# Input rows loaded at once, the residual's store moved, output rows straight from the residual

## The reference

```python
h = x + concat(rmsnorm(fox), rmsnorm(conv), rmsnorm(nsa), rmsnorm(gmlp)) @ w_out
y = h + square(relu(rmsnorm(h) @ w_ff1)) @ w_ff2
```

## Time and profile before

| | |
|---|---|
| median of the runs | 3586.47 us (3577.64, 3598.64, 3586.47) |
| the profiled execution | 3587.85 us, its span 3586.0 us |
| mean granted TensorE clock | 0.972 of full |
| busy: TensorE, VectorE, ScalarE, GpSimd | 3298.0, 1469.9, 1019.8, 206.5 us |
| the first barrier | TensorE's first product at 59.26 us |
| the last barrier | VectorE's first copy behind it at 3563.27 us |

### The profile page before, as it was taken

How to read it: one execution, slowest core, us unless ns; L and a number is a source line. 1 busy time by engine, 2 the same in 40 slices (tenths; PEclk the granted TensorE clock), 3 DMA queues, 4 the chain that set the end, 5 groups by cost and what they waited for, 6 DMA issues and landing times.

```text
span 3586.0 us, 55381 instructions
## 1 busy us (share of the span) xinstructions
PE 3298.0 (92%) x22246; PEld 1888.7 (53%) x22450; DVE 1469.9 (41%) x2767; ACT 1019.8 (28%) x1802; POOL 206.5 (6%) x136
## 2 busy tenths in 40 slices
PE   5999978888799999999989998889887999999998
PEld 3555556666544444444445554566664444444444
DVE  4875553333454321232168665433335533113321
ACT  2112334444433210221102232344444332013211
POOL 0211100000100000000002111000002000000000
PEclk9999979999999999999999998999998999999999
DMA  6432242342221121123143324334222112111322
GB/s 192 153 102 76 90 150 85 120 142 69 78 92 47 54 58 41 41 58 90 48 138 107 101 76 127 111 107 137 103 84 90 47 53 65 47 30 47 81 75 79
DMA packets 379859, 313.02 MB, mean 87 GB/s; under 512 B 125597, under 2 KB 362810, under 8 KB 372538
## 3 DMA queue, kind: packets, MB, share of 16 engines
q1 hardware_dynamic: 372234, 209.13, 20.7%
q0 software_dynamic: 7424, 101.19, 7.6%
HBM read 264.87 MB, written 50.46 MB: 88 GB/s over the span
## 4 chain that ended last, share of the span: by engine, by line
PE 82%; DVE 6%; ACT 3%; SPq 3%; issue 3%; DMA 2%; POOL 0%; POOLq 0%; DVEq 0%; ACTq 0%
PE PS L943 43%; PE PS L1058 10%; PE PS L1318 5%; PE PS L1339 4%; PE PS L972 3%; PE PS L1209 3%; PE PS L1033 2%; PE PS L1357 1%; PE PS L1388 1%; PE PS L1255 1%; DVE arena L1890 1%; ACT arena L1622 1%; PE PS L1216 1%; DVE arena L2179 1%; PE PS L1108 1%
## 5 line engine op out<-in xcount | busy, mean ns | idle before, releaser
L943 PE MATMUL PS<-arena 128*128 128x512 bf16 (+1 forms) x9882 | 1538.7, 316 | 10.4
L943 PEld LDWEIGHTS PS<-arena 128*128 128x128 bf16 x10080 | 753.4, 98 | 794.7
L1058 PE MATMUL PS<-arena 128*128 128x512 f32 (+3 forms) x1152 | 477.6, 570 | 0.0
L1499 ACT ACTIVATE arena<-arena 128x1024 bf16<-128x1024 f32 (+1 forms) x112 | 145.4, 1300 | 1095.7 <-PE PS L943 1075.4
L1058 PEld LDWEIGHTS PS<-arena 128*128 128x128 f32 (+1 forms) x1152 | 208.3, 184 | 236.6 <-issue 203.6
L2460 DVE TENSOR_TENSOR arena<-PS,arena 128x1088 f32<-128x1088 f32 (+1 forms) x48 | 62.0, 1292 | 654.8 <-PE PS L943 631.4
L2184 DVE TENSOR_REDUCE arena<-PS 128x1 f32<-128x1024 f32 (+5 forms) x192 | 138.8, 724 | 368.2 <-PE PS L1321 367.6
L1318 PE MATMUL PS<-arena 128*128 128x512 f32 (+3 forms) x576 | 236.6, 519 | 10.5 <-ACT arena L1631 8.8
L2484 DVE SCALAR_TENSOR_TENSOR arena<-PS,arena 128x1088 f32<-128x1088 f32 x64 | 82.7, 1292 | 350.9 <-PE PS L943 350.5
L1339 PE MATMUL PS<-arena 128*128 128x64 f32 x1632 | 215.9, 278 | 0.0
L1339 PEld LDWEIGHTS PS<-arena 128*128 128x128 f32 x1632 | 203.8, 197 | 8.4 <-issue 5.2
(11 more groups left out here) (334 smaller groups left out, 2880.7 us busy)
## 6 DMA issues: line engine op xcount, KB each, us to landing
arena<-in_w_ff SPq DMA_DIRECT2D x64, 512.0 KB, 4.1
arena<-in_w_ff SPq DMA_DIRECT2D x32, 1024.0 KB, 5.9
arena<-in_cache_nsa_kv SPq DMA_DIRECT2D x256, 64.0 KB
x_s<-arena SPq DMA_DIRECT2D x24, 544.0 KB, 3.5
arena<-x_s SPq DMA_DIRECT2D x2, 4352.0 KB, 12.9
arena<-in_w_in SPq DMA_DIRECT2D x4, 2048.0 KB, 14.5
arena<-in_w_out SPq DMA_DIRECT2D x16, 512.0 KB, 4.0
arena<-in_w_in SPq DMA_DIRECT2D x12, 512.0 KB, 5.8
```

What stands on the lines that cost most here:

```text
L943: last = mm(PS[:, 1536 * k + a:1536 * k + a + wd], ww[:, c, :], xx[:, c, a:a + wd], start=c == 0 and n == 0, stop=c == blocks - 1 and n == 2)
L1058: last = mm(PS[0:r, c * 512:c * 512 + b - a], XNT[:, j, t * P:t * P + r], Wt[:, j, a:b], start=j == 0, stop=j == KD - 1)
L1499: run(WH[k][:, 0:blocks, :], src[k][:, 0:blocks, :], ACT.Copy).then_inc(S["w_hi"], 1)
```

## The change

- Nine buffers `XS` take the two `XS` and the two `XO`. The input tiles are issued without a wait: tiles 0 to 3 right behind the constants, tiles 4 to 8 behind the page table's DMAs. `quad_s` is written first among these and read back after tile 8. The norm gains and the four gate weights follow.
- The constants have a semaphore of their own, `const_in`, on which TensorE and VectorE begin. `loaded_once` (288) is waited for by GpSimd and by VectorE's index tables, which now stand behind the reductions of the squares.
- SP arrives at the first barrier before it stores the residual; the eight stores are the first that it issues behind it.
- At the end TensorE transposes directly out of `XT` into four pairs of PSUM banks. ScalarE evicts the first half of a tile, VectorE the second (`row_odd`), and SP stores the tile out of its own buffer. No store is waited for before the last.

```diff
-        XS = [lo.take(DM) for _ in range(2)]
-        XO = [lo.take(KD * P, k=KD, n=P) for _ in range(2)]
+        XS = [lo.take(DM) for _ in range(QT + 1)]
...
         def _(sp):
-            sp.dma_start(const, A["consts"]).then_inc(loaded_once, 16)
+            sp.dma_start(const, A["consts"]).then_inc(const_in, 16)
+
+            def row_in(t):
+                src = A["x_prompt"][0, t * P:(t + 1) * P, :] if t < QT else A["x_sample"].rearrange("b t d -> (b t) d")
+                sp.dma_start(XS[t][0:P if t < QT else NS, :], src).then_inc(S[f"row_in{t}"], 16)
+
+            for t in range(4):
+                row_in(t)
+            sp.dma_start(quad_s.unsqueeze(2), ...).then_inc(quad_out, 16)
             sp.dma_start(pages, A["page_table"].rearrange("b j -> (b j)").unsqueeze(0)).then_inc(loaded_once, 16)
-
             for j in range(NPG):
                 r = slice(j * (P // NPG), (j + 1) * (P // NPG))
                 sp.dma_start(block_rows[r, :], ...).then_inc(loaded_once, 16)
-            sp.dma_start(quad_s.unsqueeze(2), ...).then_inc(quad_out, 16)
+            for t in range(4, QT + 1):
+                row_in(t)
             sp.wait_ge(quad_out, 16)
             sp.dma_start(piece_rows[:, 0:4], quad_s.rearrange("(g n) r -> (n r) g", g=4)).then_inc(loaded_once, 16)
...
-            over_tiles(sp, row_in, between={5: lambda: (norm_in(first), gates_in(0, first))})
-            gates_in(1, first)
+            norm_in(first)
+            for f in range(2):
+                gates_in(f, first)
...
             sp.wait_ge(S["row_ev"], QT + 1)
+            arrive(sp, "sp")
             for n in range(KD):
                 store_residual(n)
-            arrive(sp, "sp")
...
-            over_tiles(sp, row_out)
+            for t in range(QT + 1):
+                dst = ...
                 sp.wait_ge(S["row_ev"], t + 1)
+                sp.wait_ge(S["row_odd"], t + 1)
+                sp.dma_start(dst, XS[t][0:P if t < QT else NS, :]).then_inc(S["row_out"], 16)
...
         def _(pe):
-            pe.wait_ge(loaded_once, 304)
+            pe.wait_ge(const_in, 16)
+            for t in range(QT + 1):
+                k, r = t % 2, rows_of(t)
+                pe.wait_ge(S[f"row_in{t}"], 16)
+                if t >= 2:
                     pe.wait_ge(S["row_ev"], t - 1)
...
-            def row_out(t, k, m):
+            for t in range(QT + 1):
                 r = rows_of(t)
-                pe.wait_ge(S["row_cp"], t + 1)
-                if not (isinstance(t, int) and t < 2):
-                    pe.wait_ge(S["row_ev"], t - 1)
+                if t >= 4:
+                    pe.wait_ge(S["row_ev"], t - 3)
+                    pe.wait_ge(S["row_odd"], t - 3)
                 for j in range(KD):
-                    at = (2 * k + j // 4) * 512 + (j % 4) * P
-                    last = tr(PS[0:r, at:at + P], XO[k][:, j, 0:r], ident)
+                    at = (2 * (t % 4) + j // 4) * 512 + (j % 4) * P
+                    last = tr(PS[0:r, at:at + P], XT[:, j, t * P:t * P + r], ident)
                 last.then_inc(S["row_T"], 1)
...
         def _(act):
-            def row_out(t, k, m):
-                r = rows_of(t)
+            for t in range(QT + 1):
+                r, at = rows_of(t), t % 4 * 1024
                 act.wait_ge(S["row_T"], t + 1)
-                if not (isinstance(t, int) and t < 2):
-                    act.wait_ge(S[f"row_out{k}"], 16 * m)
-                run(XS[k][0:r, 0:512], PS[0:r, 1024 * k:1024 * k + 512], ACT.Copy)
-                run(XS[k][0:r, 512:1024], PS[0:r, 1024 * k + 512:1024 * k + 1024], ACT.Copy).then_inc(S["row_ev"], 1)
+                run(XS[t][0:r, 0:512], PS[0:r, at:at + 512], ACT.Copy).then_inc(S["row_ev"], 1)
...
         def _(dve):
-            dve.wait_ge(loaded_once, 304)
+            dve.wait_ge(const_in, 16)
             V.tensor_copy(identb, ident)
             V.tensor_copy(cnegb, C("cneg"))
             V.tensor_copy(wnegb, C("wneg"))
+            ...
+            each_tile(row_squares)
+            dve.wait_ge(loaded_once, 288)
             rows = KVC[:, 0:NB]
...
-            def row_cp(t, k, m):
-                ...
-                V.tensor_copy(XO[k][:, :, 0:r], XT[:, :, cols(t)]).then_inc(S["row_cp"], 1)
-
-            over_tiles(dve, row_cp)
+            for t in range(QT + 1):
+                r, at = rows_of(t), t % 4 * 1024 + 512
+                dve.wait_ge(S["row_T"], t + 1)
+                V.tensor_copy(XS[t][0:r, 512:DM], PS[0:r, at:at + 512]).then_inc(S["row_odd"], 1)
...
         def _(pool):
-            pool.wait_ge(loaded_once, 304)
+            pool.wait_ge(loaded_once, 288)
```

More of the change, by code:

```diff
@@ L510, in arrive @@
             e.sem_clear(go[who])
[L512 to L533, removed]
         SUMS_OF = {3: [(1, 0), (1, 1)], 4: [(1, 2), (2, 0)], 5: [(2, 1), (2, 2)], 6: [(3, 0), (3, 1)], 7: [(3, 2)]}
@@ L886, in _ @@
                 arrive(sp, "sp")
-            def row_out(t, k, m):
+            for t in range(QT + 1):
+                dst = O["y_prompt"][0, t * P:(t + 1) * P, :] if t < QT else O["y_sample"].rearrange("b t d -> (b t) d")
                 sp.wait_ge(S["row_ev"], t + 1)
[L891 to L896, removed]
-            over_tiles(sp, row_out)
+                sp.wait_ge(S["row_odd"], t + 1)
+                sp.dma_start(dst, XS[t][0:P if t < QT else NS, :]).then_inc(S["row_out"], 16)
             for f in range(2):
@@ L902, in _ @@
             sp.wait_ge(x_out, 128 * (layers + 1))
-            sp.wait_ge(S["row_out0"], 16 * 5)
-            sp.wait_ge(S["row_out1"], 16 * 4)
+            sp.wait_ge(S["row_out"], 16 * (QT + 1))
         @block.tensor
@@ L923, in row_T @@
                     at = (2 * k + j // 4) * 512 + (j % 4) * P
-                    last = tr(PS[:, at:at + r], XS[k][0:r, j * P:(j + 1) * P], ident[0:r, 0:r])
+                    last = tr(PS[:, at:at + r], XS[t][0:r, j * P:(j + 1) * P], ident[0:r, 0:r])
                 last.then_inc(S["row_T"], 1)
-            over_tiles(pe, row_T)
             arrive(pe, "pe")
@@ L1800, in _, with add_square, row_squares @@
             V.tensor_copy(wnegb, C("wneg"))
+            def add_square(n, total, parts, times=0):
+                if n == 0:
+                    return
+                dve.wait_ge(S["sq_ready"], KD * times + n + 1)
+                if n >= 2:
+                    dve.wait_ge(S["sq_added"], (KD - 1) * times + n - 1)
+                V.tensor_tensor(total, total, parts[n % 2], ALU.add).then_inc(S["sq_added"], 1)
+            def row_squares(t, k, m):
+                dve.wait_ge(S["sq_ready"], t + 1)
+                V.reduce_sum(SQA[:, cols(t)], SQT[k][:, :, 0:rows_of(t)].rearrange("p k n -> p n k"), AX).then_inc(S["sq_added"], 1)
+            each_tile(row_squares)
+            dve.wait_ge(loaded_once, 288)
             rows = KVC[:, 0:NB]
@@ L2516, in _ @@
                 arrive(dve, "dve")
-            def row_cp(t, k, m):
-                r = rows_of(t)
-                if not (isinstance(t, int) and t < 2):
-                    dve.wait_ge(S["row_T"], t - 1)
-                V.tensor_copy(XO[k][:, :, 0:r], XT[:, :, cols(t)]).then_inc(S["row_cp"], 1)
-            over_tiles(dve, row_cp)
+            for t in range(QT + 1):
+                r, at = rows_of(t), t % 4 * 1024 + 512
+                dve.wait_ge(S["row_T"], t + 1)
+                V.tensor_copy(XS[t][0:r, 512:DM], PS[0:r, at:at + 512]).then_inc(S["row_odd"], 1)
         @block.gpsimd
```

32 lines of the change are left out of this document (3 added, 29 removed).

## The result

The changed kernel takes 3562.99 us, the median of 8 runs (3559.37 to 3573.6), beside 3586.99 for the kernel before in 8 runs (3577.64 to 3598.64). The ratio, estimated from all runs of both, is 0.9938, with a 95% interval of 0.9921 to 0.9954: 22 us or 0.62% faster, 16 to 28 us by the interval (the two medians differ by 24.0). The forecast was 3558 with a range of 3544 to 3572. The profiled execution of the changed kernel took 3559.37 us, its span 3557.6 at a mean granted clock of 0.970.

What follows compares the result with a forecast made beforehand. Chains of waits, not busy time, were taken to bound the 59 us before TensorE's first product and 23 us after the last barrier. 3587.85 - 22.9 (start) - 7.0 (end) = 3558 us, range 3544 to 3572.

Steps and rivals of the forecast that it cites:

- The head of the start: Start: first transpose at 9.0, tile 0 handed over at 11.0, ScalarE then pacing 2.1 us a tile.
- Tile 4: Start: small table packets at 240 a microsecond delay this tile's load, pace 3.2 us late; other bound 0.
- Index arithmetic and stores: Start: VectorE's index arithmetic adds 1.6 us to the path; SP's other issues before the barrier cost nothing.
- The stores behind the barrier: Layer 1's start: loads issued 8.2 us later, thin spare of 1.8 and 0.7 us; cost taken as 0.
- The second rival: Behind the first barrier: loads behind the stores come late, VectorE's convolution starts late; at most 8.2 us, 3566; chance 0.12.
- The end: After the last barrier: direct transposes, two-engine eviction and unhindered outputs end the span at 3579, a gain of 7.0.
- my two limits: End: transposes plus eviction give 3578.9; bandwidth, 4.45 MB at 0.40 MB/us from 3565.9, gives 3578.3 and half a microsecond.
- if issues queue as the stores did: End: lower case, SP's output issues queue like the residual stores, gain 5 instead of 7.0.
- The transposes' clock: End: two slow tiles, then seven at full clock, 4.0 + 7.6 us, transposes ending at 3574.8.
- The third rival: End: transposes stay at 1.2 GHz, nine tiles at 1.98 us, gain only 0.9, total 3564; chance 0.07.
- The body: Layers between start and end: TensorE's products and the layers' order untouched, change taken as 0.
- the fourth rival: Long products: mean granted clock falls, 0.01 less costing 34 us; at 0.960 the time is 3599; chance 0.04.

Runs made afterwards that it cites:

- tiles first: Changed kernel with all nine input tiles issued ahead of the page table's DMAs instead of four; 3558.1 us (0.9926), in a second set 3557.6 (0.9923).
- two kernels: Changed kernel with nine tiles ahead of the tables, 3558.1 us; and with tables behind the gate weights too, index arithmetic on GpSimd behind the barrier, 3566.06 us.
- quad_last: Changed kernel with only the write of `quad_s` (512 elements, DRAM to DRAM) moved behind the sample tile; single run 3570.1 us.
- quad_to_sbuf: Changed kernel, block-row loads behind the tiles, the 512 elements sent to unused SBUF ahead of tile 4, real `quad_s` write last; single run 3569.69 us.

## Why the prediction was right, and where it was off

**The head of the start: right.** First transpose at 8.90 (9.0 forecast), handed over at 10.88 (11.0), 2.07 us a tile (2.1), VectorE the last to arrive, 1.3 us from there to the first product.

**Tile 4: mechanism right, size off.** This is the step that failed. I took the tables' small packets at 240 a microsecond and got a pace 3.2 us late; it was 6.9 (26.19 at ScalarE, beside 19.29 in tiles first). The row was the wrong one because it counted packets in a stretch with no long load behind them. It was also used short: the sum has 6.4 us, 1,536 elements at 240, where the 1,697 packets of the row took 7. The runs put in its place: of the 6.9 us, 3.4 to 3.8 for the DRAM destination of the 512 elements, 1.1 to 2.2 for the block rows, and 2.0 that stay with the elements in SBUF, 0.9 of it TensorE's fallen clock (which my sum had, with 2.0 for that tile) and the rest for the elements themselves and the page list's row. I had no bound on that side at all: both of mine assumed that long transfers run at 0.40 MB/us once the small ones are through. The first product stood at 40.2 instead of 36.4, a gain of 19.1 instead of 22.9.

**Index arithmetic and stores: right.** The arithmetic cost 1.6 us on the path (37.31 to 38.91), as forecast. Costing SP's own arrival at nothing held, but with less cover than I thought of: the gate weights took SP 11.57 us to issue. The last was issued at 32.9, and SP was then held by the tiles to 35; with the tiles in time it is SP that arrives last.

**The stores behind the barrier: right, by a narrow margin.** 4.7 us gained against a price of 0 for what stands behind them. I had SP's loads 8.2 us later; 49.87 to 57.9 is 8.0, and in after the eight stores took SP 8.50. The token weights were issued by 80.89, 40.7 us from the first product instead of 31.1, so 9.6 later, and of the 1.8 us of spare 0.4 was left ahead of the convolution at 81.25. It did not wait for SP, nor did the tables' first use. The second rival did not occur in after, and two kernels show it: at 2.20 us it is absorbed, at 7.12 it costs 6.3.

**The end: 5.7 instead of 7.0.** Of my two limits the bandwidth's was the one that holds: first issue at 3543.30, 2.8 us after TensorE's start, as forecast (2.7). But 3557.6 - 3543.3 = 14.3 us passed from the first issue to the end, beside the 12.9 that I had (1.3 + 11.1 + 0.5). By the windows the bytes ran from 3544.0 to about 3556.2, with a lull between two early tiles (139 GB/s in the half microsecond from 3545.5) and a falling rate at the end (303, 221 and 49 GB/s in the half microseconds from 3555), and more than a microsecond passed behind them. SP's issues meanwhile took up to 1.16 us each at a full queue, and the last came at 3551.89. That these issues cost anything is not shown, since the DMA engines' share was 1.00 from 3547 on. The case "if issues queue as the stores did" was 5. In the rate I was right: 395 and 401 GB/s. (By the page's 358 my total would have been 3559.3 and not 3559.5.) The Trainium skill, DMA: Bandwidth & Descriptors, Specifications, puts HBM at about 358 GB/s per core; these transfers ran above it, as the stores of the earlier trace rows did.

**The transposes' clock: right.** The third rival had them stay at 1.2 GHz. They alone ran from 3540.5 on, and the granted clock was 0.68 in the microsecond from 3544 and 1.00 from 3545, a tile then every 0.87 us. The Trainium skill, TensorE: Matmul & The Clock Gate, Part 4, says that the full clock does not engage for transposes; this trace disagrees, as that of before did.

**The body: right as 0.** The mean granted clock was 0.970 in after and the fourth rival had no occasion. The sum was made against one execution; by medians, 3586.99 - 24.8 = 3562.2 would have been the time with the true terms, and 3562.99 was measured. The forecast missed by 5.0 us: 3.8 of the start and 1.3 of the end; the base, an execution 0.9 over the median, and 0.8 that start and end do not account for cancel, which is luck. With the spread of the start itself, 16.7 to 19.1 between pairs of profiles, none of these is good to better than a microsecond or two.

## What to carry to other kernels

Put the long loads that the first engine needs ahead of every element-wise transfer on the same queue, above all one that writes to DRAM; count not its packets alone but what the long load behind it then gets. When a barrier is shortened by moving issues behind it, follow the same queue on to the next release: some 2 us of lateness were absorbed there, 7 gave back 6.3 where moving the tables further back had won 2.0. Cut the span at two fixed instructions before comparing profiles: what the start and the end gave could be read to a microsecond or two, while the body moved by up to 17 between runs.

## What the hardware showed that I had not expected

Behind a DRAM write of 512 single elements, a tile in 4 KB packets moved at 78 to 86 GB/s for 3 us while the DMA engines' share was 0.58 to 1.02; with the same elements into SBUF, 263 and 344 GB/s in the two microseconds from 16. The write itself took 8.3 us from issue to its use in before, with little behind it, 16.3 in after, 14.7 in quad_last and 19.3 in tiles first, with tiles beside it, and 6.5 in quad_to_sbuf, where it came last. SP's issue of one long transfer took 0.5 us at an empty queue (four tiles in 2.09) and up to 2.95 at a full one (four gate weights in 11.57, 5.94 or 15.01, by what stood ahead of them), so that SP's own time becomes the bound although it only issues.
